# One accumulated tile instead of eight in the layer normalisation: the channel sums of a hybrid decoder kernel

## What is computed

```python
def layer_norm(t, g, b, eps=NORM_EPS):
    mu = jnp.mean(t32, axis=-1, keepdims=True)
    var = jnp.mean(jnp.square(t32 - mu), axis=-1, keepdims=True)
    y = (t32 - mu) * lax.rsqrt(var + eps)
    return (y * g + b)

# in each layer, from proj = rms_norm(h) @ w_in
a = glu(glu_in); a = causal_depthwise_conv(a, conv_w[l], conv_b[l])
a = jax.nn.silu(layer_norm(a, conv_ln_g[l], conv_ln_b[l]))
y_conv = a @ w_pw[l] + b_pw[l]
o = diff_attention(q, k, v, lam); y_attn = rms_norm(o, subln[l]) * (1.0 - lam_init)
merged = sigmoid(g_conv) * y_conv + sigmoid(g_attn) * y_attn
h = h + merged @ w_o[l]
h = h + square(relu(rms_norm(h) @ w_up[l])) @ w_down[l]
```

## Time and profile before

| | us |
|---|---|
| three runs, median | 1908.7 |
| lowest and highest | 1901.85, 1911.63 |
| the profiled execution, its own time | 1910.18 |
| its span, first to last instruction | 1908.4 |
| TensorE busy in the span | 1853.2 |
| VectorE busy | 1237.2 |
| GpSimd busy | 1093.9 |
| ScalarE busy | 562.2 |

### The profile page before, as it was taken

One profiled execution on the slowest core, in us unless ns is written; L12 is line 12 of the kernel. 1 busy time (PEld: TensorE's weight loads), 2 busy tenths in 40 slices (PEclk: granted clock), 3 DMA queues, 4 the chain that ended last, 5 costly groups with the idle time before them and its releaser, 6 DMA issues. The chain is left out here.

```text
span 1908.4 us, 34269 instructions
## 1 busy us (share of the span) xinstructions
PE 1853.2 (97%) x12950; PEld 1677.2 (88%) x12950; DVE 1237.2 (65%) x1821; ACT 562.2 (29%) x1723; POOL 1093.9 (57%) x1112
## 2 busy tenths in 40 slices
PE   7999989989999999999999999999899999999999
PEld 7999878878999999999999998888678778888887
DVE  6998988866664443333477889899776644444443
ACT  3135665524412210101011156655252122010100
POOL 2656354242666666666656664433537777667664
PEclk9999999989999999999999999999999999999999
DMA  4221011011322222223232211110214222222231
GB/s 173 88 89 67 23 67 45 23 67 45 134 88 89 88 89 89 88 89 103 100 122 89 88 60 53 49 64 23 72 42 153 88 88 88 102 96 89 88 110 67
DMA packets 23870, 156.37 MB, mean 82 GB/s; under 512 B 2896, under 2 KB 3280, under 8 KB 6096
## 3 DMA queue, kind: packets, MB, share of 16 engines
q1 hardware_dynamic: 21744, 147.01, 21.9%
q10 hardware_dynamic: 2016, 7.86, 1.1%
HBM read 150.59 MB, written 4.26 MB: 81 GB/s over the span
## 5 line engine op out<-in xcount | busy, mean ns | idle before, releaser
L619 PE MATMUL psum<-u,w_hi 128*128 128x264 f32 (+1 forms) x4480 | 915.4, 316 | 27.2 <-DMA identb<-identb 12.2
L619 PEld LDWEIGHTS psum<-u,w_hi 128*128 128x128 f32 x4480 | 681.7, 190 | 83.3 <-issue 14.8
L514 POOL TENSOR_TENSOR w_lo<-w_raw,w_hi 128x512 fp32r<-128x512 f32 x440 | 628.1, 1457 | 9.2
L619 PE MATMUL psum<-u,w_lo 128*128 128x264 f32 (+1 forms) x2240 | 567.3, 314 | 0.0
L619 PEld LDWEIGHTS psum<-u,w_lo 128*128 128x128 f32 x2240 | 370.2, 190 | 25.3
L679 PE MATMUL psum<-w_hi,u 128*128 128x256 f32 (+1 forms) x1856 | 337.4, 284 | 2.0 <-POOL w_lo L521 1.9
L511 POOL TENSOR_TENSOR tick<-ones 128x1 f32<-128x1 f32 x110 | 23.0, 209 | 504.6 <-PE psum L619 504.6
L459 DVE SCALAR_TENSOR_TENSOR psum<-xg,pvec,psum 128x512 f32<-128x512 f32 x440 | 300.0, 750 | 4.3 <-DVE xg L1332 2.2
L679 PEld LDWEIGHTS psum<-w_hi,u 128*128 128x128 f32 (+1 forms) x1856 | 265.4, 173 | 10.2 <-POOL w_lo L521 2.4
L679 PE MATMUL psum<-w_lo,u 128*128 128x256 f32 (+1 forms) x928 | 259.8, 280 | 0.0
L521 POOL TENSOR_TENSOR w_lo<-w_raw,w_hi 128x128 fp32r<-128x128 f32 x384 | 173.2, 492 | 92.3 <-DVE raw L1173 49.0
(11 more groups left out here) (183 smaller groups left out, 2045.5 us busy)
## 6 DMA issues: line engine op xcount, KB each, us to landing
w_raw<-w_slabs SPq DMA_DIRECT2D x136, 1024.0 KB, 4.8
h<-x_t SPq DMA_DIRECT2D x4, 528.0 KB, 7.6
h<-x_t ACTq DMA_DIRECT2D x1, 2112.0 KB, 8.2
h_spill<-h ACTq DMA_DIRECT2D x8, 264.0 KB, 2.0
h<-h_spill ACTq DMA_DIRECT2D x1, 2112.0 KB, 8.4
out<-h SPq DMA_DIRECT2D x8, 256.0 KB, 2.0
rows<-rows ACTq DMA_DIRECT2D x2, 512.0 KB, 3.8
pvec<-pvecs ACTq DMA_DIRECT2D x2, 156.5 KB, 3.1
```

The costliest lines, as they stand in the source:

```text
L514: last = nc.gpsimd.tensor_tensor(w_lo[:, b, c:c + SLAB // 4], w_raw[:, b, c:c + SLAB // 4], w_hi[:, b, c:c + SLAB // 4], ALU.subtract)
L619: last = nc.tensor.matmul(psum[:, 2 * slot + j, 0:n], w[:, b, cut], src[:, part, kc, at0:at0 + n], start=(kc == 0 and m == 0), stop=(kc == ...
```

## The change

1. The last channel tile is added on VectorE too (one more addition of 512 columns in `ln_sums`), so TensorE sums one tile for the mean instead of two.
2. VectorE adds up the squares: `add_square(i)` adds square `i` to the running sum in `ln_t`, seven additions a layer, placed between the subtractions. It gives the buffers back (`sq_used`) and at the end raises `sq_summed`.
3. TensorE sums one tile for the variance. The hook that does it stands after gate 9 instead of after gate 8, and the hook with the transposes of `y` after gate 10 instead of after gate 9.
4. On VectorE the last `subln` stands behind the eviction of the variance, instead of ahead of gate 8's eviction.

```diff
-                channel_sums(layer, ln_ready, layer + 1, [r_inv2[:], conv[:, NT - 1, :]], st_full)
+                partition_sums(layer, ln_ready, layer + 1, r_inv2)
...
                 def squares_summed():
-                    for i in range(NT):
-                        pe.wait_ge(squared, layer * NT + i + 1)
-                        channel_sums(layer, None, 0, [ln_sq[:, i % 4, :]], st_full if i == NT - 1 else sq_used, begins=i == 0, ends=i == NT - 1)
-                a_slabs(layer, S_GATE + 4, A_GATE + 8, 1, u, None, hooks=[squares_summed, last_y])
+                    partition_sums(layer, sq_summed, layer + 1, ln_t)
+                a_slabs(layer, S_GATE + 4, A_GATE + 8, 1, u, None, hooks=[lambda: None, squares_summed, last_y])
...
-                        act.wait_ge(sq_used, layer * (NT - 1) + i - 3)
+                        act.wait_ge(sq_used, layer * (NT - 2) + max(1, i - 4))
...
-                        chain.mark(V.tensor_reduce(r_inv2[:, 0:META], conv[:, 0:NT - 1, 0:META].rearrange("p c m -> p m c"), AX_X, ALU.add))
+                        chain.mark(V.tensor_reduce(r_inv2[:, 0:META], conv[:, :, 0:META].rearrange("p c m -> p m c"), AX_X, ALU.add))
                     dve.wait_ge(v_chain, chain.value())
-                    announce(dve, V.tensor_tensor(r_inv2[:, META:T], r_inv2[:, META:T], conv[:, NT - 2, META:T], ALU.add), ln_ready, layer + 1)
+                    link(V.tensor_tensor(r_inv2[:, META:T], r_inv2[:, META:T], conv[:, NT - 2, META:T], ALU.add))
+                    announce(dve, V.tensor_tensor(r_inv2[:, META:T], r_inv2[:, META:T], conv[:, NT - 1, META:T], ALU.add), ln_ready, layer + 1)
+
+                def add_square(i):
+
+                    dve.wait_ge(squared, layer * NT + i + 1)
+                    a = ln_sq[:, 0, lo:lo + n] if i == 1 else ln_t[:, lo:lo + n]
+                    ins = V.tensor_tensor(ln_t[:, lo:lo + n], a, ln_sq[:, i % 4, lo:lo + n], ALU.add)
+                    if i < NT - 1:
+                        announce(dve, ins, sq_used, layer * (NT - 2) + i)
+                    else:
+                        announce(dve, ins, sq_summed, layer + 1)
...
                 for i in range(NT):
                     announce(dve, V.tensor_tensor(conv[:, i, lo:lo + n], conv[:, i, lo:lo + n], ln_mean[:, lo:lo + n], ALU.subtract), centred, layer * NT + i + 1)
-                subln(layer, HEADS - 1)
+                    if i > 1:
+                        add_square(i - 1)
+                add_square(NT - 1)
                 gate(layer, EARLY_GATES)

                 dve.wait_ge(st_full, layer * 4 + 3)
                 announce(dve, V.tensor_scalar(row(ln_mean[:], layer), st_ps(layer), 1.0 / D, NORM_EPS, ALU.mult, ALU.add), var_ready, layer + 1)
+                subln(layer, HEADS - 1)
                 dve.wait_ge(dev_ready, layer + 1)
```

More of the change, by code:

```diff
@@ L365, in build @@
         glu_sig, glu_out = sem("glu_sig"), sem("glu_out")
-        conv_head, centred, squared, sq_used = (sem(x) for x in ("conv_head", "centred", "squared", "sq_used"))
+        conv_head, centred, squared, sq_used, sq_summed = (sem(x) for x in ("conv_head", "centred", "squared", "sq_used", "sq_summed"))
         var_ready, dev_ready = sem("var_ready"), sem("dev_ready")
@@ L657, in partition_sums @@
                 last.then_inc(st_full, 1)
-            def channel_sums(layer, ready, value, srcs, done, begins=True, ends=True):
-                lo, n, k = span(layer)
-                n //= k
-                if ready:
-                    pe.wait_ge(ready, value)
-                for x, src in enumerate(srcs):
-                    for j in range(k):
-                        last = nc.tensor.matmul(psum[:, ST_BANK[j], 0:n], ones[:], src[:, lo + j * n:lo + j * n + n],
-                                                start=begins and x == 0, stop=ends and x == len(srcs) - 1)
-                last.then_inc(done, 1)
             def b_tile(layer, n, b, t, half):
```

## The result

The change made the kernel slower: 1930.2 us (median of four runs, 1928.4 to 1930.6) against 1909.7 (four runs, 1901.9 to 1911.6). The ratio is 1.0109, with a 95% interval from 1.0082 to 1.0135, so between 15.7 and 25.8 us.

What follows compares the result with a forecast made beforehand. It took VectorE's chain to gate 9's eviction, which gate 11 on TensorE awaits with 2.6 us slack, as the bound. Both layers summed to +14.1 to +15.8, taken as +15: median 1924, own range 1920 to 1927, full range 1912 to 1931.

Steps and rivals of the forecast that it cites:

- rival (b): Clock bites harder: gate 10 slow beyond its cover, gate 11 starts slow too; +18 to +24, 1927 to 1932; chance 0.22.
- The bound and the slack: Gate 11 on TensorE waits for VectorE's eviction of gate 9; slack 2.6 us, any longer VectorE chain stops TensorE.
- What TensorE saves, 13.3 us: Fewer mean and variance sums on TensorE in both layers: 13.3 us less work, counting only with nothing else in the way.
- The last channel on VectorE, hidden: One more VectorE addition, about 0.7 us, and one eviction behind it; hidden, as TensorE comes to the mean later.
- The additions: VectorE stands 4 us for the second square, then twelve steps of 0.74; layer 0 squares summed at 471.9 if undisturbed.
- The contact: GpSimd's split beside VectorE's additions slows them: +5.0 us in layer 0, from 0 to 6.1; summed squares at 476.9.
- From the sum to gate 11: Layer 0: 1.1 us to the variance's eviction, 10.4 of VectorE chain; gate 9 evicted at 488.5, gate 11 +6.2.
- The clock: TensorE's clock falls to 0.50 after its wait: variance sums +0.9 us in layer 0; gate 10's slowing stays hidden.
- gate 12's wait: TensorE waits at gate 12 for VectorE's eviction of gate 10: 0.65 us in layer 0, 0.7 in layer 1.
- The sum: Layer 0 +6.9 to 7.8 us, layer 1 +7.2 or 8.0; together +14.1 to +15.8, taken as +15.
- Rival (a), no contact: VectorE's additions miss GpSimd's split and keep to 0.74: +2.0 and +2.2, with clock up to +6; 1913 to 1915; chance 0.17.
- Rival (c), TensorE's saving counts: Gate 9 evicted before TensorE is through with gate 10, so the whole saving counts: -13.3 us, 1895.4; chance 0.04.

Runs made afterwards that it cites:

- No split: The changed kernel without GpSimd's split of the one slab behind gate 9 in each layer: 1919.3 us, ratio 1.0055 to the kernel before.
- the combined kernel: The changed kernel with ScalarE's squares and root ahead of its sigmoids and the last subln moved behind the reciprocal: 1911.2 us, ratio 1.0003 to the kernel before.
- Late sub-normalisation: The changed kernel with the last subln behind the second channel step, gate 10 evicted right behind gate 9, y transposes one tile later: 1927.3 us, ratio 1.0075.
- all-gates kernel: The kernel "combined with gate 9 early", with y transposes a gate tile later and gate 11 evicted behind subln, gates 12 and 13 later: 1900.9 us, ratio 0.9952.
- the kernel with it alone: The kernel before with only the last channel's addition moved to VectorE, so TensorE sums one tile for the mean: 1910.9 us, ratio 0.9995.
- with gate 9 early: The changed kernel with gate 9 evicted directly behind gate 8 and gate 10 behind Newton's step: 1929.9 us, ratio 1.0096 to the kernel before.
- squares first: The changed kernel with ScalarE taking its eight squares and the root ahead of its sigmoids: 1917.7 us, ratio 1.0045 to the kernel before.
- late split: The changed kernel with GpSimd's split behind gate 9 held back until the squares are summed: 1930.7 us, ratio 1.0087 to the kernel before.
- combined with gate 9 early: The combined kernel with gate 9 evicted ahead of the reciprocal, gate 10 behind Newton's step, gate 13 ahead of the last channel step: 1909.9 us, ratio 0.9989.

## Why the prediction was right, point by point

**The number: right in direction, short in size.** The median of 1930.2 lies inside the stated range of 1912 to 1931, but within 1 us of its end. It is outside the forecast's own 1920 to 1927 and inside the 1927 to 1932 of rival (b), whose chance was put at 0.22.

**The bound and the slack: right.** The link that decides was the eviction of gate 9 and TensorE's wait at gate 11 behind it. No split and the combined kernel shortened VectorE's chain with TensorE's work unchanged, and were faster by about 10 and 20 us by the ratios, clear of the intervals. Late sub-normalisation shortened the stages by 4.5 us, but its ratio isn't clear of that of the change. The bound holds for this order of the program: in the last kernel gate 9 is evicted ahead of the reciprocal, and the link is gone.

**What TensorE saves, 13.3 us: right.** 12.7 in the all-gates kernel. In the changed kernel the busy time fell by 3.4 us only: in the stages the matmuls took 8.1 us more at the lower clock, and between them 2.4 more.

**The last channel on VectorE, hidden: right** in the sense that no wait came ahead of the mean. That its saving on TensorE would count by itself is a thing the kernel with it alone refuted.

**The additions: right in pattern, 0.9 us off in the wait.** Predicted 4 us for the second square, measured 3.1 and 3.3. In layer 0 the squares began 0.4 us earlier (461.47, against the earlier trace rows) and the mean later, since its sum fell into a stretch of lower clock: 1.56 us from 454.56 until gate 8 at 456.12, expected 0.85. Each undisturbed step took 0.74, as estimated from the subtraction.

**The contact: right, 5.0 and 4.9 predicted, 3.6 and 5.5 measured.** The start of the split decides the size: at 469.4 it left one step for L512 and two for L514; in layer 1 one and four. The single prices come close: 2.43 beside L512 (predicted 0.74 + 1.9, though the row of before gives 2.44 in all), 1.64 to 1.66 beside L514 (1.79). In layer 0 the late start of gate 8, at the lower clock, kept the contact small: with gate 9 early that stage began at full clock, and the contact was 5.5. The errors of the two layers, 1.4 too much and 0.6 too little, partly cancel; that is luck. The rule of the page "SBUF — State Buffer", section "SBUF: two separate sides", in the Trainium skill agrees with the trace here: the additions were caught.

**From the sum to gate 11: right.** Predicted from the start of the sum to gate 9 evicted: 1.1 + 10.4, and 0.9 for the slow sum, 12.4 in layer 0; measured 12.5 (475.30 to 487.79). The sum took 2.16 us to its eviction (475.30 to 477.46). In layer 1 10.95 + 0.8, measured 12.1. Counted from the mean's start, gate 11 began 5.9 us later than before in layer 0 (forecast 6.2 to 7.1; the smaller contact) and 8.2 later in layer 1 (6.5 to 7.3; the larger).

**The clock: right at the sums, a term too small at gate 11.** Gate 10 was slow until about 479, less long than thought, and stayed hidden. But gate 11, behind its own wait of 3.5 us, started at the lower clock as well: 7.49 us to gate 12 (495.33) instead of 5.84. Rival (b) named that. I had only 0.65 us at this place, for gate 12's wait, which didn't come, since gate 10 was evicted by then. So 1.65 stands for 0.65 in layer 0. In layer 1 gate 11 took 7.06 instead of 5.62, and 1.2 of that is left at the end of the stage, for 0.7.

**The sum.** Stage of layer 0: +7.6, predicted 6.9 to 7.8. Stage of layer 1: +9.4, predicted 7.2 to 8.0. There the contact was 0.6 above its term (5.5 for 4.9), the chain behind the sum 0.3, and gate 11's slow start 0.5. Together +17.0 instead of +15.

**What was not foreseen: +3.6 us between the stages.** In fourteen profiles of kernels whose code there differs by no more than one addition, that piece took from 888.3 (squares first) to 897.3 us (late split); in the three whose squares TensorE sums 888.5, 890.1 and 890.3. Of the 3.6 us, TensorE's idle time has 1.2 and its busy time 2.4, for the same number of matmuls. The clock stood at its lower level there for 10.2 us in before, 17.1 in after and 30.7 in late split; after has one more such stretch at 1298 us and a longer one at 1349, both in the second layer's attention. One microsecond of the idle time can be put to a row. VectorE and GpSimd, before and then after:

```profile
608.76 0.71 DVE L1110 TENSOR_TENSOR sumsq<-sumsq,sq 128x528 f32<-128x528 f32 x1 [1.44 <-ACT u L861]
608.76 6.08 POOL L514 TENSOR_TENSOR w_lo<-w_raw,w_hi 128x512 fp32r<-128x512 f32 x4
```

```profile
616.00 1.84 DVE L1096 TENSOR_TENSOR sumsq<-sumsq,sq 128x528 f32<-128x528 f32 x1 [1.44 <-ACT u L847]
615.98 5.97 POOL L514 TENSOR_TENSOR w_lo<-w_raw,w_hi 128x512 fp32r<-128x512 f32 x4
```

The two engines come to this place with the same distance in both kernels, within 0.02 us. Before, VectorE's step ran at its 0.71; after, GpSimd's began 0.02 us ahead of it, the step took 1.84, and TensorE waited 0.8 us for what follows. A tie that falls the other way is not the change's cost. What sets the stretches of lower clock wasn't settled either; one profile of each kernel doesn't tell how much of the 3.6 is the change's and how much is the execution's. Here the 1924 of the forecast and the 1930 of the result part.

**Rival (a), no contact**: its time was 1913 to 1915; the kernel without the split gave 1919, with stages 5.1 and 3.3 us above before, where the rival had up to 6 for both. The clock was the part it had too small. **Rival (c), TensorE's saving counts**: its condition was named rightly (squares ahead of the sigmoids), but not fully. With that alone the time was 1917.7; it took the sub-normalisation's place, five evictions and the transposes too to reach 1900.9, and its 1895.4 was not reached. Its other condition, the summed squares by 463.6 (8.7 us after the mean), wasn't met and wasn't needed: they came 13.1 us after it, and that was early enough, since gate 9's eviction no longer stood behind the sub-normalisation, the reciprocal and Newton's step. The rule of the Trainium skill that stands beside it ("Perfetto Trace Analysis", "Identifying the Most-Contended Engine") pointed at the engine where time could be had in the end: TensorE leads by its weight loads too, by which that page judges it (88%). For this change it gave the wrong sign.

## What to carry to other kernels

Work taken from the busiest engine counts only when nothing that it waits for becomes later: find the next hand-over behind the edit, here the eviction two tiles back, and compare its slack (2.6 us) with what the other engine gets to do. Work moved on to VectorE needs a place beside which no split of GpSimd runs, and moving either of them hands the contact on to whatever stands next. When a change of this kind comes out slow, look whether evictions of finished tiles stand behind long chains that don't need to be first: such moves turned 1911 into 1901. Taking out some of the waits brought little (1909.9); with nearly all of them gone, the lower clock behind them went too.

## What the runs showed of the hardware that I had not expected

- Very small VectorE steps pay the full price beside GpSimd: 0.17 us of work took 1.21 (five columns), even one with a single tensor as input (L1129). A run of such steps is worse to place there than one large one: the first four steps of `subln` in late split lost 3.8 us together, an addition of 528 columns after the change 0.95.
- The reciprocal, 528 columns from SBUF, did not: 3.45 us beside L514 and 3.45 without it (combined with gate 9 early, and after). The step behind it did, 1.85 instead of 0.71. Timeline of VectorE and below it GpSimd, combined with gate 9 early, layer 0:

```profile
469.00 3.45 DVE L1423 RECIPROCAL ln_rs<-ln_t 128x528 f32<-128x528 f32 x1
472.48 1.85 DVE L1118 TENSOR_TENSOR ln_t<-ln_rs 128x528 f32<-128x528 f32 x1
```

```profile
468.70 5.07 POOL L514 TENSOR_TENSOR w_lo<-w_raw,w_hi 128x512 fp32r<-128x512 f32 x4
```

- A wait of 3.1 to 3.5 us on TensorE was followed by matmuls at the lower clock (after: 0.66 over the 5 us from 487, against 1.00 from 479 to 484). In the combined kernel gate 11, behind waits of 3.1 and 2.9 us, with the transposes took 1.4 and 2.8 us longer than at full clock.
- Two steps that start together can fall either way: at 608.76 in before the VectorE step kept its 0.71 us, at 616.00 in after the same step took 1.84 behind a GpSimd step that began 0.02 us sooner.
